# Gated attention in joined units of two blocks, with a second set of buffers, and all scaling of the weights on GpSimd

## The chip, the cores and the metric

The kernel runs on one core of a Trainium2 chip. The metric is the time of one execution in microseconds (us), as the device measures it. A core has five engines, each with its own stream of instructions that it works off in order: TensorE (PE; its weight loads are PEld), VectorE (DVE), ScalarE (ACT), GpSimd (POOL) and SyncE (SP, which issues the DMAs). They meet only at semaphores.

## What is computed

The program runs a transformer of several layers on 512 tokens of width 1024. The change touches one stage, the gated attention of the second layer (`nsa_mixer` in the reference): 16 query heads of width 64 in two groups, and three branches with a gate each. The compressed branch (32 averaged keys) is computed beside the other two, which are full causal attention here, since the selection keeps all blocks of 512 tokens and the window is 512 wide:

```
s_s = jnp.einsum('bqghd,bgqkd->bghqk', qb, k_g) * scale
p_s = masked_softmax(s_s, valid_s[:, :, None]).astype(v_g.dtype)
o_s = jnp.einsum('bghqk,bgqkd->bqghd', p_s, v_g)
...
out = gb[..., 0:1] * o_c + gb[..., 1:2] * o_s + gb[..., 2:3] * o_w
```

## The kernel before

The stage is one loop on each engine, written out by hand, over the list `NSA`: m (8 pairs of heads), x (0 selected, 1 window), b (4 blocks of 128 queries; block b sees b + 1 tiles of 128 keys, so a tile of it is 128 x (b + 1) wide). Two heads (a = 0, 1) go side by side. An iteration over m holds eight blocks, numbered n.

What happens to block n, step by step: TensorE multiplies queries and keys into two of the banks 0 to 3 (L1085, `pe_nsa_logits`); VectorE adds the mask, scales and takes the maximum into `exps` (L2267, `dve_masks`); ScalarE takes exponentials in place and their sum (L1618, `act_exps`); VectorE inverts the sums (L2446) and scales head 0's tile by the inverse and the gate (L2449, both in `dve_nsa_scale`); GpSimd scales head 1's (L2652, `pool_nsa`); TensorE transposes both tiles into banks 4 and 5 (L1100, `pe_nsa_turn`, three steps after the logits); ScalarE copies them to `weights_c` (L1712, `act_nsa_turned`); and when the four blocks of an (m, x) are through, TensorE multiplies them with the values into bank 6 (L1112, `pe_nsa_values`).

Once in an iteration the compressed branch is threaded in, by fixed places in the loop: logits into bank 7 (L1125), on VectorE their maximum and difference (L2461 to L2465, `dve_cmp_logits`), the exponential on ScalarE, the weights on VectorE (L2474 to L2479, `dve_cmp_weights`), two transposes into bank 7 (L1136), a copy to `p_cmpT` on ScalarE (`act_take`), and the values (L1146) into bank 6. The queries of the next m are rotated too: a matmul into bank 7 (L729, `pe_rope`) and three operations on VectorE (L2159 to L2164). Bank 7 is a channel: each writer waits (`emptied7`) until the reader of what was written before has read it. Bank 6 goes to `u` by a copy on ScalarE after the second values of an iteration.

Buffers: the logits banks are reused every second block, so logits n wait for the masks of n - 2 (`c_masked`); `exps` holds one tile for each b and head, so the mask of block n waits for the transposes of n - 4 (`c_t_done`); the transposes wait for ScalarE's copies of the block before (`c_turned0`, `c_turned1`) and for the scaled tiles (`c_scaled`, `c_scaled_1`).

Of the kernel before, what the change touches and what calls it, by code (L numbers as in the profile page):

```python
# [311 lines left out]
def buffers(k):  # L312
# [55 lines left out]
    with ExitStack() as st:  # L368
        exp_buffers(k, st)
# [89 lines left out]
NSA = [(m, x, b) for m in range(8) for x in range(2) for b in range(NB)]  # L459
DA = [(h, b) for h in range(4) for b in range(NB)]  # L460
# [589 lines left out]
def pe_nsa(k):  # L1050


    pe, s = k.pe, k.s
    pe.wait_ge(s["combined"], 2 * (CH_C // 2 + N_C // 2 - 1))
    for step in range(len(NSA) + 5):
        if step < len(NSA):
# [6 lines left out]
        if 0 <= step - 3 < len(NSA):  # L1063
# [24 lines left out]

def pe_nsa_turn(k, n):
    pe, s = k.pe, k.s  # L1090
    m, x, b = NSA[n]
    for a in range(2):
        if n:
            pe.wait_ge(s[f"c_turned{a}"], n)
        if (n, a) == (1, 0):
            pe_keep(k, k.bank[4], 8)
        pe.wait_ge(s[("c_scaled", "c_scaled_1")[a]], n + 1)
        e = sized_tile(k, n, b, a)
        for j in range(b + 1):
            ins = pe.transpose(k.bank[4 + a][:, j * P:(j + 1) * P], e[:, j * P:(j + 1) * P], k.const("ident"))  # L1100
        ins.then_inc(s["c_t_done"], 1)
# [576 lines left out]
def act_nsa(k):  # L1678
    act, s = k.act, k.s
    for step in range(len(NSA) + 5):  # L1680
        m, at = divmod(step, 8)
        n = step - 3
        if 0 <= n < len(NSA):
            act_nsa_turned(k, n)
        if step < len(NSA):
            act_exps(k, step, NSA[step][2], "c_masked", "c_exp_done", sized_tile)
        if m < 8 and at == 0:
            act.wait_ge(s["cmp_shifted"], m + 1)
            act.activation(k.pc, k.pc, ACT.Exp).then_inc(s["cmp_exp"], 1)
        if m < 8 and at == 4:  # L1690
            act_take(k, k.ch7, ("cmpT", m), k.pcT.rearrange("p h q -> p (h q)"), k.ch7.bank[:, 0:2 * P])
        n = step - 4
        if 0 <= n < len(NSA) and n % 8 == 7:
            act_take(k, k.ch6, ("nsa", n // 8), k.u[:, n // 8, :], k.ch6.bank)
# [11 lines left out]
def act_nsa_turned(k, n):  # L1706
    act, s = k.act, k.s
    m, x, b = NSA[n]
    nsa_weights_free(k, act, n)
    for a in range(2):  # L1710
        act.wait_ge(s["c_t_done"], 2 * n + a + 1)
        act.copy(k.ceT[x][a][:, 0:b + 1, b * P:(b + 1) * P],  # L1712
                 k.bank[4 + a][:, 0:P * (b + 1)].rearrange("p (j t) -> p j t", t=P)).then_inc(s[f"c_turned{a}"], 1)
# [700 lines left out]
def dve_nsa(k):  # L2414
    dve, s = k.dve, k.s
    for step in range(len(NSA) + 5):
        m, at = divmod(step, 8)
        if step < len(NSA):
            free = (s["c_t_done"], 2 * (step - 4) + 1, 1) if step >= 4 else None
            dve_masks(k, step, NSA[step][2], causal(k, NSA[step][2]), "c_lg_done", "c_masked", free, SCALE, sized_tile)  # L2420
# [19 lines left out]
def dve_nsa_scale(k, n):  # L2440
# [1113 lines left out]
```

## Time and profile before

| | |
|---|---|
| median of three runs | 2269.31 us (2268.11 to 2269.79) |
| profiled execution | 2269.1 us, its span 2267.8 us |
| PE busy | 98% of the span |
| DVE, ACT, POOL busy | 59%, 25%, 9% |
| granted TensorE clock, mean | 0.999 |

A matmul's busy time includes the time until its result is out, which overlaps the next one; so a busy PE is an engine with work in flight. The stage of the change lies between 855 and 1027 us.

### The profile page before, as it was taken

What the parts mean: (1) busy time and instruction counts of PE and PEld (TensorE: products, weight loads), DVE (VectorE), ACT (ScalarE), POOL (GpSimd) and SP (SyncE); (2) the same over time, 40 slices, a digit from 0 to 9 for tenths busy, and PEclk for the clock granted to TensorE, in tenths of its full rate; (3) what the DMA queues carried; (4) which work ended last, traced back from release to release, by engine and by line L of the source; (5) the groups of instructions that cost most, each with busy time, mean ns of one, the idle gap of its engine ahead of it and who ended that gap; (6) DMA issues with size and microseconds to landing.
All of it is one profiled execution on the core that took longest, in us unless ns stands there. A gap on an engine that the chain in (4) does not pass through costs nothing.

```text
span 2267.8 us, 29576 instructions
## 1 busy us (share of the span) xinstructions
PE 2211.9 (98%) x10990; PEld 1585.1 (70%) x10990; DVE 1344.5 (59%) x3432; ACT 560.3 (25%) x1421; POOL 199.3 (9%) x210
## 2 busy tenths in 40 slices
PE   9999999999999999999999999999999999999997
PEld 7776578888888885558888888888867643333333
DVE  6777756656566667886665666767776522222224
ACT  2223431101001206772110000333572111111111
POOL 0013430000000002330000000000020011111011
PEclk9999999999999999999999999999999999999999
DMA  5211032232223320002222222232205899999997
GB/s 212 75 57 47 13 124 85 83 93 89 79 93 92 116 75 20 1 1 75 76 93 93 78 90 93 76 103 65 65 11 223 347 421 423 423 423 424 424 424 310
DMA packets 60207, 346.54 MB, mean 153 GB/s; under 512 B 9248, under 2 KB 10144, under 8 KB 42208
## 3 DMA queue, kind: packets, MB, share of 16 engines
q1 hardware_dynamic: 55360, 335.03, 39.6%
q0 software_dynamic: 3840, 6.46, 0.8%
q10 hardware_dynamic: 864, 3.15, 0.3%
q8 instruction: 90, 1.47, 0.3%
q14 instruction: 53, 0.43, 0.1%
HBM read 337.59 MB, written 17.30 MB: 156 GB/s over the span
## 4 chain that ended last, share of the span: by engine, by line
PE 86%; DMA 9%; DVE 2%; ACT 1%; issue 1%; SPq 0%; DVEq 0%; POOLq 0%; ACTq 0%
PE bank L634 30%; DMA places<-in_experts 8%; PE bank L640 8%; PE bank L647 8%; PE bank L655 8%; PE bank L3051 6%; PE bank L3059 3%; PE bank L623 2%; PE bank L1100 2%; PE bank L1085 2%; PE bank L1112 2%; PE bank L3008 1%; PE bank L729 1%; PE bank L3024 1%; PE bank L497 1%; PE bank L1307 1%
## 5 line engine op out<-in xcount | busy, mean ns | idle before, releaser
L3051 PE MATMUL bank<-places,xT 128*64 128x512 f32 x824 | 184.0, 594 | 13.9 <-DMA places<-in_experts 13.9
L3260 DVE TENSOR_SCALAR square<-bank,mt 128x256 f32<-128x256 f32 x32 | 15.5, 484 | 288.0 <-ACT rope L3163 288.0
L3051 PEld LDWEIGHTS bank<-places,xT 128*64 128x64 f32 x824 | 59.3, 137 | 133.0 <-issue 117.9
L1961 DVE TENSOR_TENSOR third<-first,bank 128x256 f32<-128x256 f32 x106 | 44.7, 421 | 150.9 <-PE bank L634 150.2
L634 PE MATMUL bank<-u,ring 128*128 128x256 f32 x540 | 130.3, 381 | 1.1 <-DVE y_ab L1995 1.1
L634 PE MATMUL bank<-h,ring 128*128 128x256 f32 x512 | 120.9, 379 | 0.0
L634 PE MATMUL bank<-h_sums,w_sum 128*128 128x256 f32 x512 | 120.9, 379 | 0.0
L2652 POOL TENSOR_SCALAR exps<-exps,small,gates 128x128 f32<-128x128 f32 (+1 forms) x64 | 56.4, 882 | 657.6 <-DVE small L2446 657.6
L634 PEld LDWEIGHTS bank<-u,ring 128*128 128x128 f32 x540 | 101.2, 190 | 17.8 <-issue 3.3
L634 PE MATMUL bank<-u_mlp_sums,w_sum 128*128 128x256 f32 x480 | 113.4, 379 | 0.0
L634 PE MATMUL bank<-u_mlp,ring 128*128 128x256 f32 x480 | 113.4, 379 | 0.0
L1491 ACT ACTIVATE h<-relu 128x512 f32<-128x512 f32 x64 | 40.3, 630 | 273.8 <-DVE relu L2145 250.0
L634 PEld LDWEIGHTS bank<-h,ring 128*128 128x128 f32 x512 | 97.3, 190 | 13.2
L634 PEld LDWEIGHTS bank<-h_sums,w_sum 128*128 128x128 f32 x512 | 97.3, 190 | 13.2
L634 PE MATMUL bank<-exps,w_sum 128*128 128x256 f32 x432 | 102.1, 379 | 0.0
L634 PEld LDWEIGHTS bank<-u_mlp_sums,w_sum 128*128 128x128 f32 x480 | 91.2, 190 | 12.4
L634 PEld LDWEIGHTS bank<-u_mlp,ring 128*128 128x128 f32 x480 | 91.2, 190 | 12.4
L1618 ACT ACTIVATE exps<-exps,small 128x128 f32<-128x128 f32 (+3 forms) x160 | 88.9, 561 | 35.1 <-DVE small L2267 34.6
L3059 PE MATMUL bank<-places,square 128*64 128x512 f32 x392 | 90.0, 598 | 2.4 <-DMA places<-in_experts 2.4
L634 PEld LDWEIGHTS bank<-exps,w_sum 128*128 128x128 f32 x432 | 81.4, 190 | 11.9 <-issue 1.2
L1394 ACT COPY first<-bank 128x256 f32<-128x256 f32 x44 | 16.4, 372 | 275.4 <-PE bank L634 259.4
L640 PE MATMUL bank<-u,ring 128*128 128x256 f32 x312 | 75.8, 382 | 0.0
(556 smaller groups left out, 4406.2 us busy)
## 6 DMA issues: line engine op xcount, KB each, us to landing
places<-in_experts SPq DMA_DIRECT2D x56, 2048.0 KB, 35.1
ring<-in_dense SPq DMA_DIRECT2D x216, 512.0 KB, 4.2
places<-in_experts SPq DMA_DIRECT2D x40, 1024.0 KB, 26.2
x<-in_experts SPq DMA_DIRECT2D x12, 1024.0 KB, 37.8
w<-in_experts SPq DMA_DIRECT2D x10, 1024.0 KB, 32.1
consts<-in_experts SPq DMA_DIRECT2D x10, 1024.0 KB, 32.9
x<-in_experts SPq DMA_DIRECT2D x4, 2048.0 KB, 33.5
consts<-in_consts SPq DMA_DIRECT2D x1, 2310.5 KB, 16.4
```

The costliest lines, as they stand in the source:

```text
L623: ins = pe.matmul(bank, w[:, j, :], x(j), start=i == 0, stop=i == 3)
L634: ins = pe.matmul(bank, w[:, j, :], x(j), start=j == 0, stop=j == 3)
L640: ins = pe.matmul(part[2], a12[:, j, :], tile(2 * j + 1)[:, 0:HT], start=j == 0, stop=j == 3)
L647: ins = pe.matmul(part[4], a22[:, j, :], t4[:, j, :], start=j == 0, stop=j == 3)
L655: ins = pe.matmul(part[3], s4[:, j, :], tile(2 * j + 1)[:, HT:T], start=j == 0, stop=j == 3)
L1085: pe.matmul(logits_bank(k, n, a)[:, 0:P * (b + 1)], k.yc[r, CQ + m, b * P:(b + 1) * P], k.yc[r, (KS, KW)[x], 0:P * (b + 1)], start=True, s ...
L1100: ins = pe.transpose(k.bank[4 + a][:, j * P:(j + 1) * P], e[:, j * P:(j + 1) * P], k.const("ident"))
L1112: ins = pe.matmul(ch.bank[r, j * P:T], k.vcs[x][:, j, r], k.ceT[x][a][:, j, j * P:T], start=False, stop=x == 1 and j == NB - 1)
L1618: act.activation(e, e, ACT.Exp, bias=neg[:, a:a + 1], scale=-1.0, accum_out=total[:, a:a + 1]).then_inc(s[done], 1)
L2652: pool.tensor_scalar(e, e, inv[:, 1:2], k.gt[:, b, q:q + 1], ALU.mult, ALU.mult).then_inc(s["c_scaled_1"], 1)
L3051: ins = k.pe.matmul(bank[a * CAP:(a + 1) * CAP, :], xT[:, kk % 4, kk // 4, :], w[:, (2 * (kk % 2) + a) * EH:(2 * (kk % 2) + a + 1) * EH], ...
L3059: ins = k.pe.matmul(bank[a * CAP:(a + 1) * CAP, :], hT[:, c % 2, c // 2, :], w[:, c % 2 * D + a * T:c % 2 * D + (a + 1) * T], start=c == 0 ...
```

## The change

Three things. First, on TensorE blocks 0 and 1 of each (m, x) are one unit (`NSA_UNITS`), with blocks 2 and 3 as units of their own: their logits go side by side into one pair of banks (block 1 at column 128), and their transposes likewise. An iteration has six steps instead of eight, and every lag (three steps to the transposes, four to the values) counts units. Second, `exps` is ten tiles wide instead of six and holds two sets of a group's tiles (`nsa_tile`), so a mask waits for the transposes of n - 8. Third, GpSimd scales the tiles of both heads, one after the other, and VectorE only inverts. The masks of a unit now wait for all logits of it.

```
@@ pe_nsa @@
-    for step in range(len(NSA) + 5):
+    for step in range(len(NSA_UNITS) + 4):
...
-        m, at = divmod(step, 8)
+        m, at = divmod(step, 6)
...
-        if m < 8 and at == 4:
+        if m < 8 and at == 3:
             pe_cmp_turn(k, m)
-        if m < 7 and at == 5:
+        if m < 7 and at == 3:
             pe.wait_ge(s["scaled"], SCALED["c"] + CQ + m + 2)
             pe_rope(k, k.ch7, ("cq", m + 1), k.yc[:, CQ + m + 1, :])
-        if m < 8 and at == 6:
+        if m < 8 and at == 4:
             pe_cmp_values(k, m)
-        if 0 <= step - 4 < len(NSA) and NSA[step - 4][2] == NB - 1:
-            pe_nsa_values(k, step - 4)
+        if step >= 4 and (step - 4) % 3 == 2:
+            pe_nsa_values(k, NSA_UNITS[step - 4][-1])
@@ pe_nsa_turn @@
+    for a in range(2):
+        for n in NSA_UNITS[u]:
+            m, x, b = NSA[n]
+            if u and n == NSA_UNITS[u][0]:
+                pe.wait_ge(s[f"c_turned{a}"], n)
...
+            pe.wait_ge(s[("c_scaled", "c_scaled_1")[a]], n + 1)
@@ act_nsa @@
+        if 0 <= step - 3 < len(NSA_UNITS):
+            for n in NSA_UNITS[step - 3]:
+                act_nsa_turned(k, n)
+        if step < len(NSA_UNITS):
+            for n in NSA_UNITS[step]:
+                act_exps(k, n, NSA[n][2], "c_masked", "c_exp_done", nsa_tile)
...
-        if m < 8 and at == 4:
+        if m < 8 and at == 3:
             act_take(k, k.ch7, ("cmpT", m), k.pcT.rearrange("p h q -> p (h q)"), k.ch7.bank[:, 0:2 * P])
@@ dve_nsa @@
-            free = (s["c_t_done"], 2 * (step - 4) + 1, 1) if step >= 4 else None
+            unit = NSA_UNITS[nsa_unit(step)]
+            free = (s["c_t_done"], nsa_turns(step - 8, 0), len(unit)) if step >= 8 else None
+            dve.wait_ge(s["c_lg_done"], 2 * (unit[-1] + 1))
@@ dve_nsa_scale @@
     k.inverted.append(own.link(dve.reciprocal(inv, total)))
-    dve.wait_ge(own.sem, k.inverted[n])
-    e, q = sized_tile(k, n, b, 0), 6 * m + 1 + x
-    dve.tensor_scalar(e, e, inv[:, 0:1], k.gt[:, b, q:q + 1], ALU.mult, ALU.mult).then_inc(s["c_scaled"], 1)
@@ pool_nsa @@
-        e, q = sized_tile(k, n, b, 1), 6 * m + 4 + x
         pool.wait_ge(k.dve_own.sem, k.inverted[n])
-        pool.tensor_scalar(e, e, inv[:, 1:2], k.gt[:, b, q:q + 1], ALU.mult, ALU.mult).then_inc(s["c_scaled_1"], 1)
+        for a in range(2):
+            e, q = nsa_tile(k, n, b, a), 6 * m + 3 * a + 1 + x
+            pool.tensor_scalar(e, e, inv[:, a:a + 1], k.gt[:, b, q:q + 1], ALU.mult, ALU.mult).then_inc(s[("c_scaled", "c_scaled_1")[a]], 1)
```

The change moves instructions on every engine; three places follow. The first is TensorE in the middle of an iteration. Before, from the transposes of block 1 on: L1100 are transposes, L1136 the compressed ones, L1085 logits, L729 the rope.

```order
L1100 MATMUL bank<-consts,exps 128x128
L1100 MATMUL bank<-consts,exps 128x128 [waits c_scaled_1,c_turned1]
L1100 MATMUL bank<-consts,exps 128x128
L1136 MATMUL bank<-consts,p_cmp 128x128 [waits emptied7,cmp_weights]
L1136 MATMUL bank<-consts,p_cmp 128x128
L1085 MATMUL bank<-y_c 128x256 [waits c_masked]
L1085 MATMUL bank<-y_c 128x256
L1100 MATMUL bank<-consts,exps 128x128 [waits c_scaled,c_turned0]
L1100 MATMUL bank<-consts,exps 128x128 x2
L1100 MATMUL bank<-consts,exps 128x128 [waits c_scaled_1,c_turned1]
L1100 MATMUL bank<-consts,exps 128x128 x2
L729 MATMUL bank<-y_c,consts 128x512 [waits emptied7,scaled]
```

Of the changed kernel, the same place (L1125 transposes, L1161 the compressed ones, L731 the rope, L1137 the values, L1109 logits):

```order
L1125 MATMUL bank<-consts,exps 128x128 [waits c_scaled,c_turned0]
L1125 MATMUL bank<-consts,exps 128x128 [waits c_scaled]
L1125 MATMUL bank<-consts,exps 128x128
L1125 MATMUL bank<-consts,exps 128x128 [waits c_scaled_1,c_turned1]
L1125 MATMUL bank<-consts,exps 128x128 [waits c_scaled_1]
L1125 MATMUL bank<-consts,exps 128x128
L1161 MATMUL bank<-consts,p_cmp 128x128 [waits emptied7,cmp_weights]
L1161 MATMUL bank<-consts,p_cmp 128x128
L731 MATMUL bank<-y_c,consts 128x512 [waits emptied7,scaled]
L1137 MATMUL bank<-weights_c,y_c 64x512 [waits c_turned1,c_turned0]
L1137 MATMUL bank<-weights_c,y_c 64x512
L1137 MATMUL bank<-weights_c,y_c 64x384 x2
```

The rope now stands directly behind the compressed transposes, which fill the same bank 7, with no logits or transposes between them, and the values stand behind the rope.

The second place is ScalarE at the same point. Before (L1712 copies of transposed tiles, L1618 exponentials of two heads, L1419 the copy of `p_cmpT`):

```order
L1712 COPY weights_c<-bank 128x2x128 [waits c_t_done] x2
L1618 ACTIVATE exps,small<-exps,small 128x128 [waits c_masked] x2
L1419 COPY p_cmpT<-bank 128x256 [waits filled7]
L1712 COPY weights_c<-bank 128x3x128 [waits c_t_done] x2
L1618 ACTIVATE exps,small<-exps,small 128x256 [waits c_masked] x2
```

Now (L1743, L1649, L1444):

```order
L1743 COPY weights_c<-bank 128x128 [waits c_t_done,c_weighed]
L1743 COPY weights_c<-bank 128x128 [waits c_t_done]
L1743 COPY weights_c<-bank 128x2x128 [waits c_t_done] x2
L1649 ACTIVATE exps,small<-exps,small 128x128 [waits c_masked] x2
L1649 ACTIVATE exps,small<-exps,small 128x256 [waits c_masked] x2
L1444 COPY p_cmpT<-bank 128x256 [waits filled7]
L1444 COPY u<-bank 128x512 [waits filled6]
```

The copy of `p_cmpT` came behind one block's copies and one block's exponentials; it now comes behind those of two blocks.

The third place is VectorE from the mask of block 2 to the reciprocal of block 1. Before (L2267 the masks, L2446 reciprocal, L2449 the scaling, L2474 to L2479 the compressed weights), the last rows of it:

```order
L2446 RECIPROCAL small<-small 128x2 [waits c_exp_done]
L2449 TENSOR_SCALAR exps<-exps,small,gates 128x128 [waits dve_chain]
L2474 TENSOR_TENSOR p_cmp<-p_cmp,consts 128x256 [waits cmp_exp]
L2475 TENSOR_REDUCE small<-p_cmp 128x8 [waits dve_chain]
L2476 TENSOR_SCALAR small<-small 128x8 [waits dve_chain]
L2477 RECIPROCAL small<-small 128x8 [waits dve_chain]
L2478 TENSOR_TENSOR small<-small,gates 128x8 [waits dve_chain]
L2479 TENSOR_TENSOR p_cmp<-p_cmp,small 128x256 [waits dve_chain]
L2267 ISA exps,small<-bank,consts 128x512 [waits c_lg_done,c_t_done]
L2267 ISA small 128x1
L2267 ISA exps,small<-bank,consts 128x512 [waits c_lg_done,c_t_done]
L2267 ISA small 128x1
```

Now (L2298, L2479, L2504 to L2509):

```order
L2479 RECIPROCAL small<-small 128x2 [waits c_exp_done]
L2504 TENSOR_TENSOR p_cmp<-p_cmp,consts 128x256 [waits cmp_exp]
L2505 TENSOR_REDUCE small<-p_cmp 128x8 [waits dve_chain]
L2506 TENSOR_SCALAR small<-small 128x8 [waits dve_chain]
L2507 RECIPROCAL small<-small 128x8 [waits dve_chain]
L2508 TENSOR_TENSOR small<-small,gates 128x8 [waits dve_chain]
L2509 TENSOR_TENSOR p_cmp<-p_cmp,small 128x256 [waits dve_chain]
L2298 ISA exps,small<-bank,consts 128x512 [waits c_lg_done,c_t_done]
L2298 ISA small 128x1
L2298 ISA exps,small<-bank,consts 128x512 [waits c_lg_done,c_t_done]
L2298 ISA small 128x1
L2479 RECIPROCAL small<-small 128x2 [waits c_exp_done]
```

Here the scalings are gone and nothing else is moved on VectorE; what moves is TensorE beside it. The transposes of block 1, which wait for the last reciprocal, by way of the scaling, used to have the values of the group before ahead of them on TensorE; in the joined unit they stand ahead of those values.

## Rows read from the trace of the kernel before

**Rows 1.** The page's table of busy time and share of the span by engine.
```profile
PE 2211.9 (98%) x10990; PEld 1585.1 (70%) x10990; DVE 1344.5 (59%) x3432; ACT 560.3 (25%) x1421; POOL 199.3 (9%) x210
```

**Rows 2.** Busy time by engine in the stage: stretch, length, PE, PEld, DVE, ACT, POOL, clock, DMA.
```profile
855.00:1027.00 172.00, 159.66 (x1012) 91.91 (x1011) 132.44 (x493) 126.63 (x408) 56.41 (x64) 1.00 0.01 4
```

**Rows 3.** The chain of waits over one iteration: start, us, what.
```profile
917.02 1.05 PE bank L1125 x8
...
920.16 0.97 PE bank L1100 x6
921.14 0.85 PE bank L1085 x4
921.98 1.03 PE bank L1100 x8
923.01 1.06 PE bank L1085 x4
...
924.57 2.31 PE bank L1112 x16
...
929.88 1.10 PE bank L729 x2
...
932.84 0.89 PE bank L1146 x8
...
937.89 1.05 PE bank L1125 x8
```

**Rows 4.** Groups by line, the stage and its seven later iterations: count, busy, mean, idle before.
```profile
L2449 DVE TENSOR_SCALAR exps<-exps,small,gates 128x128 f32<-128x128 f32 (+1 forms) x64 | 28.7, 449 | 2.4
...
L1100 PE MATMUL bank<-consts,exps 128*128 128x128 f32 x278 | 44.5, 283 | 8.2 <-DVE exps L2449 7.2
```

**Rows 5.** VectorE in order of time: start, us, instruction, idle before in brackets.
```profile
922.12 0.56 DVE L2267 CUSTOM_DVE_ANT_0 exps<-bank,consts 128x384 f32<-128x384 f32 x1 [0.76 <-PE bank L1085]
...
923.08 0.16 DVE L2446 RECIPROCAL small<-small 128x2 f32<-128x2 f32 x1
...
923.54 0.42 DVE L2474 TENSOR_TENSOR p_cmp<-p_cmp,consts 128x256 f32<-128x256 f32 x1
...
925.44 0.68 DVE L2267 CUSTOM_DVE_ANT_0 exps<-bank,consts 128x512 f32<-128x512 f32 x1
...
926.66 0.16 DVE L2446 RECIPROCAL small<-small 128x2 f32<-128x2 f32 x1
```

**Rows 6.** GpSimd in order of time, the stage and the attention stage before it.
```profile
299.18 1.82 POOL L2642 TENSOR_SCALAR exps<-exps,small 128x256 f32<-128x256 f32 x2 [2.16 <-DVE small L2340]
...
920.88 1.04 POOL L2652 TENSOR_SCALAR exps<-exps,small,gates 128x512 f32<-128x512 f32 x1 [0.41 <-DVE small L2446]
...
926.92 0.70 POOL L2652 TENSOR_SCALAR exps<-exps,small,gates 128x256 f32<-128x256 f32 x1 [2.80 <-DVE small L2446]
...
930.13 1.57 POOL L2652 TENSOR_SCALAR exps<-exps,small,gates 128x512 f32<-128x512 f32 x1 [1.13 <-DVE small L2446]
...
1019.02 2.40 POOL L2652 TENSOR_SCALAR exps<-exps,small,gates 128x256 f32<-128x256 f32 x3 [2.96 <-DVE small L2446]
```

**Rows 7.** ScalarE in order of time.
```profile
921.55 0.51 ACT L1618 ACTIVATE exps<-exps,small 128x256 f32<-128x256 f32 x1
...
922.61 1.07 ACT L1712 COPY weights_c<-bank 128x512 f32<-128x512 f32 x2
...
928.06 0.64 ACT L1712 COPY weights_c<-bank 128x256 f32<-128x256 f32 x2
928.59 0.42 ACT L1618 ACTIVATE exps<-exps,small 128x128 f32<-128x128 f32 x1
...
929.37 0.36 ACT L1419 COPY p_cmpT<-bank 128x256 f32<-128x256 f32 x1
```

**Rows 8.** Busy time by engine as above, in the first layer's attention stage; the clock follows POOL.
```profile
292.00:294.00 2.00, 2.00 (x9) 1.20 (x9) 0.69 (x3) 0.81 (x2) 2.00 (x2) 0.68 0.00 0
294.00:296.00 2.00, 2.00 (x13) 1.34 (x12) 1.30 (x6) 1.23 (x5) 1.59 (x2) 0.50 0.04 12
```

More of the change, by code:

```diff
@@ L459 @@
 NSA = [(m, x, b) for m in range(8) for x in range(2) for b in range(NB)]
+NSA_UNITS = [tuple(NB * g + b for b in blocks) for g in range(16) for blocks in ((0, 1), (2,), (3,))]
 DA = [(h, b) for h in range(4) for b in range(NB)]
@@ L1089, in pe_nsa_turn @@
[L1089 to L1101, printed above, removed]
+        if step >= 4 and (step - 4) % 3 == 2:
+            pe_nsa_values(k, NSA_UNITS[step - 4][-1])
@@ new lines, in nsa_unit, with nsa_at, nsa_turns, nsa_logits @@
+def nsa_unit(n):
+    return 3 * (n // NB) + max(0, n % NB - 1)
+def nsa_at(n):
+    return P if n % NB == 1 else 0
+def nsa_turns(n, a):
+    unit = NSA_UNITS[nsa_unit(n)]
+    return 2 * unit[0] + a * len(unit) + unit.index(n) + 1
+def nsa_logits(k, n, a):
+    return k.bank[2 * (nsa_unit(n) % 2) + a][:, nsa_at(n):]
+def pe_nsa_logits(k, u):
+    pe, s = k.pe, k.s
+    if u >= 2:
+        pe.wait_ge(s["c_masked"], 2 * (NSA_UNITS[u - 2][-1] + 1))
+    for n in NSA_UNITS[u]:
+        m, x, b = NSA[n]
+        if n % 8 == 0:
+            pe.wait_ge(s["roped"], ROPED["cq", m])
+        for a in range(2):
+            r = slice(a * HD, (a + 1) * HD)
+            pe.matmul(nsa_logits(k, n, a)[:, 0:P * (b + 1)], k.yc[r, CQ + m, b * P:(b + 1) * P], k.yc[r, (KS, KW)[x], 0:P * (b + 1)],
+                      start=True, stop=True).then_inc(s["c_lg_done"], 1)
@@ new lines, in pe_nsa_turn @@
+def pe_nsa_turn(k, u):
+    pe, s = k.pe, k.s
+    for a in range(2):
+        for n in NSA_UNITS[u]:
+            m, x, b = NSA[n]
+            if u and n == NSA_UNITS[u][0]:
+                pe.wait_ge(s[f"c_turned{a}"], n)
+            if (n, a) == (1, 0):
+                pe_keep(k, k.bank[4], 8)
+            pe.wait_ge(s[("c_scaled", "c_scaled_1")[a]], n + 1)
+            e, at = nsa_tile(k, n, b, a), nsa_at(n)
+            for j in range(b + 1):
+                ins = pe.transpose(k.bank[4 + a][:, at + j * P:at + (j + 1) * P], e[:, j * P:(j + 1) * P], k.const("ident"))
+            ins.then_inc(s["c_t_done"], 1)
@@ L1603, in sized_tile, with nsa_tile @@
     return k.eb.rearrange("p b t -> p (b t)")[:, at:at + P * (b + 1)]
+def nsa_tile(k, n, b, a):
+    at = P * (20 * (n // NB % 2) + 10 * a + b * (b + 1) // 2)
+    return k.ec[:, at:at + P * (b + 1)]
 def soft_columns(k, n):
@@ L1679, in act_nsa @@
     act, s = k.act, k.s
[L1680 to L1689, printed above, removed]
-        if m < 8 and at == 4:
+    for step in range(len(NSA_UNITS) + 4):
+        m, at = divmod(step, 6)
+        if 0 <= step - 3 < len(NSA_UNITS):
+            for n in NSA_UNITS[step - 3]:
+                act_nsa_turned(k, n)
+        if step < len(NSA_UNITS):
+            for n in NSA_UNITS[step]:
+                act_exps(k, n, NSA[n][2], "c_masked", "c_exp_done", nsa_tile)
+                if n % 8 == 0:
+                    act.wait_ge(s["cmp_shifted"], m + 1)
+                    act.activation(k.pc, k.pc, ACT.Exp).then_inc(s["cmp_exp"], 1)
+        if m < 8 and at == 3:
             act_take(k, k.ch7, ("cmpT", m), k.pcT.rearrange("p h q -> p (h q)"), k.ch7.bank[:, 0:2 * P])
-        n = step - 4
-        if 0 <= n < len(NSA) and n % 8 == 7:
-            act_take(k, k.ch6, ("nsa", n // 8), k.u[:, n // 8, :], k.ch6.bank)
+        if step >= 4 and (step - 4) % 6 == 5:
+            act_take(k, k.ch6, ("nsa", (step - 4) // 6), k.u[:, (step - 4) // 6, :], k.ch6.bank)
 def nsa_weights_free(k, eng, n):
@@ L1710, in act_nsa_turned @@
     for a in range(2):
-        act.wait_ge(s["c_t_done"], 2 * n + a + 1)
+        act.wait_ge(s["c_t_done"], nsa_turns(NSA_UNITS[nsa_unit(n)][-1], a))
         act.copy(k.ceT[x][a][:, 0:b + 1, b * P:(b + 1) * P],
-                 k.bank[4 + a][:, 0:P * (b + 1)].rearrange("p (j t) -> p j t", t=P)).then_inc(s[f"c_turned{a}"], 1)
+                 k.bank[4 + a][:, nsa_at(n):nsa_at(n) + P * (b + 1)].rearrange("p (j t) -> p j t", t=P)).then_inc(s[f"c_turned{a}"], 1)
 def act_2_among(k, i):
```

20 lines of the change are left out of this document (5 added, 15 removed).

## The prediction

> **What bounds the kernel now.** I read the page first, for who is busy, and then cut out the one stage that the diff touches. TensorE is in use for 98% of the span [rows 1], so any other engine's saving counts only where TensorE waits for that engine. The stage runs from 855 to 1027 us: 172 us, of which TensorE shows 159.7 us busy, VectorE 132.4, ScalarE 126.6, GpSimd 56.4 [rows 2]. Nothing is moved by DMA here, so no transfer can be late.
>
> The chain of waits says what TensorE does from one iteration over m to the next [rows 3]. An iteration repeats every 20.87 us (917.02 to 937.89, the compressed logits of two iterations). The reader is to see that the pieces are TensorE's own and that only one wait matters, the one that ends at 920.16: VectorE works off the compressed logits and only then scales a 384-wide tile (L2449), for which six transposes wait. Grouped over the seven iterations from 876 on, TensorE waited 7.2 us for that line, 1.03 us each time [rows 3, 4]. So there is about 1.1 us an iteration to win from waits, and the rest is TensorE's own work.
>
> **What the change removes.** Eight scalings per iteration leave VectorE. They are 28.7 us of VectorE's time over the stage, 3.6 an iteration [rows 4]; VectorE was not the bound, but the one wait above loses its last part. The doubled buffer takes away the wait of the masks for the transposes; in the trace the masks' idle time ends with the logits instead (the 0.76 us ahead of the 384-wide mask [rows 5]), so I cost that part at nothing. The cover is that transposes of the block four steps back are always issued before. The joined units save two waiting groups of logits an iteration; the joined logits have as many columns (128 + 256) as a 384-wide block, and I give them its 0.85 us.
>
> TensorE's new order per iteration, without any stall, from the pieces of [rows 3] (six transposes 0.9, two 0.3): logits of blocks 0 and 1 0.85 us, compressed logits 1.05, six transposes 0.9, values 2.31, logits 0.84, transposes 0.9, logits 1.06, transposes 1.03, logits 0.85, transposes 0.9, compressed transposes 0.3, rope 1.10, values 2.31, logits 0.84, transposes 0.9, compressed values 0.89, logits 1.06, transposes 1.03. That is 19.1 us, or 1.7 less than now.
>
> **What it moves onto the path, first place: VectorE's and GpSimd's chain for block 1.** Count from TensorE's start of logits 0 and 1. The values of the group before now stand ahead of the logits of block 2, so these start at 0.85 + 1.05 + 0.9 + 2.31 = 5.1. The mask of block 2 starts 1.0 later, at 6.1 (TensorE 921.14, mask 922.12 [rows 3, 5]). Then VectorE goes on in its order: reciprocal 0.96 after the mask's start, 0.2 for it, the compressed weights 1.90 (923.54 to 925.44), the mask of block 3 1.22 (to 926.66), the reciprocal of block 1, and GpSimd starts 0.26 after that (926.92) [rows 5, 6]. That is 6.1 + 0.96 + 0.2 + 1.90 + 1.22 + 0.26 = 10.6. GpSimd now scales both heads one after the other, 2 x 0.70 [rows 6], to 12.0. The transposes of blocks 0 and 1 end at about 12.4. TensorE could have done them by 5.1 + 0.84 + 0.9 + 1.06 + 1.03 + 0.85 + 0.9 = 10.7. The stall is 1.7 us. Today the values (2.31) stand between and hide this very chain.
>
> **Second place: the rope behind ScalarE.** The rope matmul has moved up to stand directly behind the compressed transposes. Both write bank 7, so the rope waits until ScalarE has copied p_cmpT out. ScalarE does that copy now behind the four copies of the transposed tiles of blocks 0 and 1 and behind the exponentials of two blocks; before, behind one block's of each, with logits and six transposes of TensorE's in between. From 12.4: the last three copies, about 0.1 + 0.2 + 0.64 [rows 7], to 13.3; exponentials of a 128-wide block 0.78 (928.59 to 929.37) and of a 256-wide one 1.06 (921.55 to 922.61), to 15.2; from the start of the p_cmpT copy to the rope 0.51 (929.37 to 929.88), to 15.7 [rows 3, 7]. TensorE was ready at 12.7, so this stall is 3.0 us. Queued behind the rope on TensorE are the values, the next logits and all that follows; VectorE's rope and ScalarE's copy of u wait in turn. From 15.7: rope 1.10, values 2.31, logits 0.84, transposes 0.9, compressed values 0.89, logits 1.06, transposes 1.03: the iteration ends at 23.8 instead of 20.9, so +3.0 us. The end of one iteration does not catch up: the next one's logits wait for nothing that is late.
>
> **The sum of the waits.** Six iterations (m = 1 to 6) pay 3.0 each, 18. The first has nothing to overlap and one values group less: about +1. The last has no rope, keeps the first stall and lands near today's 20. After the last logits GpSimd scales six tiles instead of the three of today's 2.40 us [rows 6]: +2.6, rounded to 3. Together +22.
>
> **The clock.** The granted clock is full in the whole stage today. It fell at a place of the same kind, in the attention stage of the first layer, where TensorE also waits between short groups: the windows from 292 show 0.68 and then 0.50, which is the 1.2 GHz level [rows 8]. Its price by those two rows is 2 x 0.32 + 2 x 0.50 = 1.6 us of full-speed work. In the new order TensorE does only six transposes and the compressed ones between 10.0 and 15.7, a longer pause than any today. I expect one such fall in each of the seven iterations with a rope; part falls into the pause itself and costs nothing, so I take 1.1 us of the 1.6, 7.7 in all.
> The Trainium skill, "TensorE: Matmul & The Clock Gate", on the HAM clock gate, says that idleness throttles the array to 1.2 GHz and that activity releases it; by that rule the clock falls here, by the stage's own rows it would hold. The trace at 292 us agrees with the page.
>
> The profiled execution took 2269.1 us (span 2267.8, 1.3 around it), 0.2 below the median of 2269.31. 2269.1 + 22 + 7.7 = 2298.8, so **2299 us**.
>
> **GpSimd's price** is the term least known. From below: 0.70 for a 256-wide tile, and three back to back in 2.40 us (the same operation) [rows 6]. From above: the attention stage's own scaling, 1.82 for two 256-wide tiles, 0.91 each, and the one of 1.57 for a 512-wide tile where VectorE ropes beside it, against 1.04 without [rows 6]. I take the lower one, since the three back to back are of this very form.
> The Trainium skill, "SBUF — State Buffer", section "Who interferes with whom", says that a VectorE instruction with two SBUF inputs and a GpSimd instruction that reads SBUF exclude each other, and whichever comes first blocks the other. By that, a compressed-weights operation could wait behind a GpSimd scaling, up to 1.04 us more in the first chain and about 7 us over the stage. The trace shows only the half of it in which GpSimd is the longer one (1.57 against 1.04); VectorE's product with two SBUF inputs at 923.54 took 0.42, no longer than its one-input neighbours [rows 5].
>
> **Rivals.**
> - Both stalls as worked out and the clock falls: 2299, by itself 2291 to 2306. Chance 0.50.
> - Both stalls, the clock holds as in today's stage: 2269.1 + 22 = 2291. For it: 1 us pauses leave the clock alone there. Against: the new pause is several times as long. 0.18.
> - GpSimd at the upper price: 0.4 more in the first chain, 0.4 more for the transposes that open the iteration, times 7, and 1.6 in the drain: +7, 2306. 0.15.
> - Faster, the other side: if ScalarE's copy of p_cmpT came in time and the first chain were covered, TensorE's 19.1 us would set the iteration: 8 x -1.7 + 3 = -11, 2258. The point of decision is 1.7 us of stalls an iteration; I find 4.7. For it speaks that VectorE, the engine behind today's wait, loses 3.6 us of work an iteration. Against it speaks the order on ScalarE. 0.09.
> - Stalls of about 1.7 us, so that the change cancels itself: 2269. 0.04.
> - The clock stays low through the rest of each iteration after the pause: 8.1 us of work at half speed, seven times: +57, about 2347. 0.04.
>
> A measurement of this kernel tells a difference from none at about 0.2%, 4.5 us. Faster 0.09, same 0.04, slower 0.87. The range takes in the first three cases with their spread: 2284 to 2310.
>
> **What would show it.** In the changed profile the iteration is near 24 to 25 us. Ahead of the rope matmul TensorE idles 2.5 to 3.5 us until ScalarE's p_cmpT copy; among the transposes of blocks 0 and 1 in the second half it idles 1 to 2 us until GpSimd; the wait for the scaling after the compressed logits is gone. VectorE's busy time in the stage falls by some 29 us and GpSimd's doubles. The granted clock dips once an iteration. The prediction is wrong if ScalarE reaches the p_cmpT copy before TensorE is through with the transposes, if GpSimd's pairs take much other than 1.4 us at 256 wide, or if the clock's share is far from 8 us.

## The result and the profile after

The changed kernel takes 2298.16 us (median of four runs, 2296.26 to 2300.51), the kernel before 2268.71 beside it. The ratio is 1.0127, with a 95% interval of 1.0114 to 1.0140: slower by 1.3%. The forecast was 2299, its range 2284 to 2310. Its profiled execution took 2297.0 us, its span is 2295.7.

The page's table of busy time, which answers to [rows 1], says that TensorE does the same number of instructions and is busy for 97% of a longer span instead of 98%, and that the scaling has gone over: VectorE has 64 instructions and 26.6 us less, GpSimd 64 and 26.3 us more.

```profile
PE 2220.9 (97%) x10990; PEld 1587.5 (69%) x10990; DVE 1317.9 (57%) x3368; ACT 562.1 (24%) x1421; POOL 225.6 (10%) x274
```

Busy time by engine in the stage, and in the two-us windows around one fall of the clock (columns as in [rows 2]). The first row answers to [rows 2], the others to [rows 8]. The stage now ends at 1056.91 instead of 1026.23, where the next matmul is one of L625 (L623 before), and its mean clock is 0.92 instead of 1.00.

```profile
855.00:1056.00 201.00, 167.53 (x1000) 93.36 (x1000) 104.71 (x428) 127.04 (x407) 82.67 (x128) 0.92 0.01 4
939.00:941.00 2.00, 0.00 (x0) 0.00 (x0) 0.00 (x0) 2.00 (x10) 2.00 (x4) 1.00 0.00 0
941.00:943.00 2.00, 1.42 (x2) 0.50 (x2) 0.00 (x0) 0.44 (x3) 0.40 (x1) 0.53 0.03 8
943.00:945.00 2.00, 2.00 (x5) 0.53 (x6) 1.23 (x2) 0.00 (x0) 0.00 (x0) 0.50 0.00 0
945.00:947.00 2.00, 2.00 (x8) 0.71 (x6) 0.15 (x1) 0.00 (x0) 0.00 (x0) 0.50 0.00 0
947.00:949.00 2.00, 2.00 (x13) 0.92 (x10) 0.00 (x0) 0.59 (x1) 0.00 (x0) 0.77 0.00 0
```

What TensorE waited for in the stage (us in total, times, longest): two causes, 19.5 and 11.0 us, hold nearly all of it. The wait of [rows 4] for the scaling after the compressed logits is gone.

```profile
PE bank L731 <- ACT p_cmpT L1444: 19.5, 7, 2.8
PE bank L1125 <- POOL exps L2683: 11.0, 9, 1.3
PE bank L1109 <- DVE small L2298: 1.3, 1, 1.3
```

TensorE in order of time over one iteration (start, us; L1150 are the compressed logits, L1125 transposes, L1109 logits, L1161 the compressed transposes, L731 the rope, L1137 the values). The reader is to see two pauses that the order of before did not have, and that the rope and the values behind the second one take 2.05 and 4.52 us, where the values at 929.06 took 2.37.

```profile
927.36 1.10 PE L1150 MATMUL bank<-k_cmp,y_c 128*128 128x64 f32 x8
928.30 0.83 PE L1125 MATMUL bank<-consts,exps 128*128 128x128 f32 x6
929.06 2.37 PE L1137 MATMUL bank<-weights_c,y_c 128*64 128x512 f32 x16
931.37 0.92 PE L1109 MATMUL bank<-y_c 64*128 64x384 f32 x4
...
935.96 0.33 PE L1125 MATMUL bank<-consts,exps 128*128 128x128 f32 x1
937.60 0.98 PE L1125 MATMUL bank<-consts,exps 128*128 128x128 f32 x5 [1.32 <-POOL exps L2683]
938.41 0.38 PE L1161 MATMUL bank<-consts,p_cmp 128*128 128x128 f32 x2
941.58 2.05 PE L731 MATMUL bank<-y_c,consts 128*128 128x512 f32 x2 [2.78 <-ACT p_cmpT L1444]
943.56 4.52 PE L1137 MATMUL bank<-weights_c,y_c 128*64 128x512 f32 x16
...
953.49 1.10 PE L1150 MATMUL bank<-k_cmp,y_c 128*128 128x64 f32 x8
```

The chain of waits through the same two places answers to [rows 3]. First place: VectorE's reciprocal, then GpSimd, then five transposes. Second place: ScalarE's copies, its eight instructions of exponentials, its copy of p_cmpT, then the rope.

```profile
936.81 0.09 DVE small L2479
...
936.98 0.57 POOL exps L2683
...
937.60 0.99 PE bank L1125 x5
...
938.62 0.82 ACT weights_c L1743 x3
939.43 1.74 ACT exps L1649 x8
941.18 0.27 ACT p_cmpT L1444
...
941.58 2.05 PE bank L731 x2
```

The compressed logits start at 876.96 in the second iteration and at 1028.76 in the eighth, so six periods are 151.80 us, 25.30 each (24.64 to 26.13), against 20.87.

### The profile page after: what moved, and what is told of

Its sections match the earlier page's. It is cut to its first block, busy times and chain, and to the rows that moved or that the text cites. A ratio compares the mean times of both kernels' runs of the same rounds, so it can differ in the third digit from the quotient of the medians.

```text
span 2295.7 us, 29545 instructions
## 1 busy us (share of the span) xinstructions
PE 2220.9 (97%) x10990; PEld 1587.5 (69%) x10990; DVE 1317.9 (57%) x3368; ACT 562.1 (24%) x1421; POOL 225.6 (10%) x274
## 4 chain that ended last, share of the span: by engine, by line
PE 86%; DMA 9%; DVE 2%; ACT 2%; issue 1%; SPq 0%; POOL 0%; DVEq 0%; POOLq 0%; ACTq 0%
PE bank L636 29%; DMA places<-in_experts 8%; PE bank L642 8%; PE bank L649 8%; PE bank L657 8%; PE bank L3082 6%; PE bank L3090 3%; PE bank L625 2%; PE bank L1137 2%; PE bank L1125 2%; PE bank L1109 2%; PE bank L3039 1%; PE bank L731 1%; PE bank L3055 1%; PE bank L499 1%
## 5 line engine op out<-in xcount | busy, mean ns | idle before, releaser
L3082 PE MATMUL bank<-places,xT 128*64 128x512 f32 x824 | 183.8, 594 | 13.6 <-DMA places<-in_experts 13.5
L2683 POOL TENSOR_SCALAR exps<-exps,small,gates 128x128 f32<-128x128 f32 (+3 forms) x128 | 82.7, 658 | 661.4 <-DVE small L2479 661.4
L636 PE MATMUL bank<-u,ring 128*128 128x256 f32 x540 | 130.3, 381 | 1.1 <-DVE y_ab L2026 1.1
L1649 ACT ACTIVATE exps<-exps,small 128x128 f32<-128x128 f32 (+3 forms) x160 | 88.8, 563 | 28.9 <-DVE small L2298 28.9
L2298 DVE CUSTOM_DVE_ANT_0 exps<-bank,consts 128x128 f32<-128x128 f32 (+3 forms) x136 | 59.1, 473 | 48.0 <-PE bank L1109 47.7
L1419 ACT COPY first<-bank 128x256 f32<-128x256 f32 x44 | 16.4, 373 | 275.3 <-PE bank L636 259.3
```

Of the source, the lines that this page charges most:

```text
L636: ins = pe.matmul(bank, w[:, j, :], x(j), start=j == 0, stop=j == 3)
L1649: act.activation(e, e, ACT.Exp, bias=neg[:, a:a + 1], scale=-1.0, accum_out=total[:, a:a + 1]).then_inc(s[done], 1)
L2298: dve.tensor_tensor_reduce(tile(k, n, b, a), logits(k, n, a)[:, 0:w], mask, -scale, 3.0e38, ALU.add, ALU.min, neg[:, a:a + 1]).then_inc(s[ ...
L2683: pool.tensor_scalar(e, e, inv[:, a:a + 1], k.gt[:, b, q:q + 1], ALU.mult, ALU.mult).then_inc(s[("c_scaled", "c_scaled_1")[a]], 1)
L3082: ins = k.pe.matmul(bank[a * CAP:(a + 1) * CAP, :], xT[:, kk % 4, kk // 4, :], w[:, (2 * (kk % 2) + a) * EH:(2 * (kk % 2) + a + 1) * EH], ...
```

## The experiments

All but one start from the changed kernel. The first four tell apart the order at the rope, the clock and GpSimd.

**Values ahead of the rope.** In the step that holds both, TensorE issues the values before the rope matmul.

```
-        if m < 7 and at == 3:
-            pe.wait_ge(s["scaled"], SCALED["c"] + CQ + m + 2)
-            pe_rope(k, k.ch7, ("cq", m + 1), k.yc[:, CQ + m + 1, :])
-        if m < 8 and at == 4:
-            pe_cmp_values(k, m)
         if step >= 4 and (step - 4) % 3 == 2:
             pe_nsa_values(k, NSA_UNITS[step - 4][-1])
+        if m < 7 and at == 3:
+            pe.wait_ge(s["scaled"], SCALED["c"] + CQ + m + 2)
+            pe_rope(k, k.ch7, ("cq", m + 1), k.yc[:, CQ + m + 1, :])
+        if m < 8 and at == 4:
+            pe_cmp_values(k, m)
```

> The changed kernel with one move on TensorE: at the fourth step of an iteration the values of the group before stand ahead of the rope instead of behind it. Theory of two stalls and the clock: the values (2.3 us) cover most of the 2.78 us for which the rope waits for the copy of p_cmpT, in six iterations of seven (the first has no values there), 14 us, and with the pause gone most of the 15 us that the lowered clock costs come back too: 2271 us, 2266 to 2277. Rival, GpSimd's doubled scaling is what costs: the rope's place does not matter, within 4 us of 2298.

It took 2274.45 us, ratio to the kernel before 1.0032 (1.0019 to 1.0044). That is 24 us off the changed kernel, of its 29. TensorE in order of time:

```profile
933.87 0.98 PE L1125 MATMUL bank<-consts,exps 128*128 128x128 f32 x5 [1.32 <-POOL exps L2683]
934.68 0.38 PE L1161 MATMUL bank<-consts,p_cmp 128*128 128x128 f32 x2
934.99 2.37 PE L1137 MATMUL bank<-weights_c,y_c 128*64 128x512 f32 x16
937.85 1.10 PE L731 MATMUL bank<-y_c,consts 128*128 128x512 f32 x2 [0.48 <-ACT p_cmpT L1444]
```

The values now fill the time in which ScalarE works, 2.3 of the 2.78 us of the wait, and rope and values run at full speed: the clock of the stage is 0.98 instead of 0.92. The first pause is as before, 1.32. So the second pause together with its clock is most of the loss. In this trace the clock falls once, from 872 to 879 us, in the first iteration: no values stand there to fill the wait, which is still 2.78. In the six others, with a pause of 1.32 and one of 0.48, it does not fall, so the first pause by itself does not bring it down.

**The copy ahead of the exponentials.** The other way to mend the same place, on ScalarE: it takes p_cmpT out before the exponentials of the next unit.

```
@@ act_nsa @@
+        if m < 8 and at == 3:
+            act_take(k, k.ch7, ("cmpT", m), k.pcT.rearrange("p h q -> p (h q)"), k.ch7.bank[:, 0:2 * P])
         if step < len(NSA_UNITS):
             for n in NSA_UNITS[step]:
                 act_exps(k, n, NSA[n][2], "c_masked", "c_exp_done", nsa_tile)
...
-        if m < 8 and at == 3:
-            act_take(k, k.ch7, ("cmpT", m), k.pcT.rearrange("p h q -> p (h q)"), k.ch7.bank[:, 0:2 * P])
```

> The changed kernel with one move on ScalarE: the copy of p_cmpT ahead of the exponentials of blocks 0 and 1 (1.85 us) instead of behind them. Theory of two stalls: the rope's wait falls from 2.78 to about 0.9 us, 7 x 1.85 = 13 us, and a part of the clock's loss, some 7 us: 2278 us, 2271 to 2286. Rival, GpSimd: the exponentials come later and nothing is won, 2298.

It took 2275.84 us, ratio 1.0038 (1.0024 to 1.0052). The wait for p_cmpT is down from 19.5 us to 7.4 (seven times, 1.05 each in the trace of this kernel), the stage's clock is 0.97: with pauses of 1.3 and 1.05 us it still falls in two of the seven iterations (at 884 and 973 us). Two orders on two engines, one result: it is the position of the rope relative to that one copy, not anything that either step costs.

**Keep the clock up in the pauses.** Both waits stay. TensorE does matmuls on constants in them, whose results nobody reads: four pairs ahead of block 1's transposes, ten pairs ahead of the rope.

```
@@ pe_nsa_turn @@
+            if n > 1 and n % 8 == 1 and a == 0:
+                pe.wait_ge(k.ch7.emptied, k.ch7.n)
+                pe_keep(k, k.ch7.bank, 4)
             pe.wait_ge(s[("c_scaled", "c_scaled_1")[a]], n + 1)
@@ pe_nsa @@
         if m < 7 and at == 3:
+            pe.wait_ge(s["c_masked"], 2 * (NSA_UNITS[step - 1][-1] + 1))
+            pe_keep(k, k.bank[2 * ((step + 1) % 2)], 10)
```

> The changed kernel with matmuls that nobody reads put into TensorE's two pauses (four ahead of the transposes of block 1, ten ahead of the rope), so that it works while it waits. Nothing else moves. Theory: the waits stay as long, and the granted clock stays full; the rope and the values behind it lose their 15.1 us of slowness over seven iterations, less up to 2 us that the fillers overrun: 2284 us, 2281 to 2288. Rival, the clock costs nothing because the waits absorb it: 2298.

It took 2283.86 us, ratio 1.0071 (1.0054 to 1.0088), 14.3 less than the changed kernel. TensorE in order of time (L499 is the filling):

```profile
933.36 1.06 PE L499 MATMUL bank<-consts 128*128 128x128 f32 x8
934.82 0.97 PE L1130 MATMUL bank<-consts,exps 128*128 128x128 f32 x5 [0.41 <-POOL exps L2688]
935.63 0.38 PE L1166 MATMUL bank<-consts,p_cmp 128*128 128x128 f32 x2
935.85 2.40 PE L499 MATMUL bank<-consts 128*128 128x128 f32 x20
938.79 1.10 PE L731 MATMUL bank<-y_c,consts 128*128 128x512 f32 x2 [0.55 <-ACT p_cmpT L1449]
939.82 2.38 PE L1142 MATMUL bank<-weights_c,y_c 128*64 128x512 f32 x16
```

The rope starts as late as before, 3.16 us after the compressed transposes (935.63 to 938.79; 938.41 to 941.58 in the changed kernel). Only the clock differs: 1.00 over the stage. The compressed logits come at 878.58, 901.59, 924.60 and so on, 23.01 apart every time. This run separates the two terms of the sum: 14.3 us of the 29.5 are clock (15.4 by the length of the stage in the two traces), the rest is waiting, the longer end of the stage included.

**Head 0's scaling back on VectorE.** The joined units and the second set stay.

```
@@ dve_nsa_scale @@
+    dve.wait_ge(own.sem, k.inverted[n])
+    e, q = nsa_tile(k, n, b, 0), 6 * m + 1 + x
+    dve.tensor_scalar(e, e, inv[:, 0:1], k.gt[:, b, q:q + 1], ALU.mult, ALU.mult).then_inc(s["c_scaled"], 1)
@@ pool_nsa @@
-        for a in range(2):
+        for a in (1,):
```

> The changed kernel with head 0's scaling back on VectorE, so that GpSimd scales one head as before; joined units and doubled buffers stay. Theory of two stalls: the chain to the transposes of block 1 loses 0.70 us on GpSimd and gains 0.35 on VectorE (the scaling of block 0 ahead of the compressed weights), 0.35 x 8 = 3 us, and the drain loses 2.6: 2293 us, 2288 to 2297; the rope's wait stays at 2.8 us. Rival, GpSimd's doubled scaling is the cost: most of the 29 us come back, under 2283.

It took 2299.76 us, ratio 1.0137 (1.0115 to 1.0159): no gain, where I had expected some 5 us (2288 to 2297). The four runs go from 2294.1 to 2303.9, so the totals alone would not tell 5 us from none; the trace does for the first pause. What TensorE waited for in the stage:

```profile
PE bank L731 <- ACT p_cmpT L1444: 19.5, 7, 2.8
PE bank L1125 <- DVE exps L2482: 11.2, 9, 1.4
```

The first pause has the same length with another name on it. GpSimd saves nothing and costs nothing there: what is late is VectorE's whole row ahead of the scaling (mask, compressed weights, mask), and whoever scales comes behind it.

**The compressed weights a step later.** That row can be shortened for block 1: VectorE works out the compressed weights in the next step of its loop, behind the mask and the reciprocal that block 1 needs.

```
@@ dve_nsa @@
-        if m < 8 and at == 2:
+        if m < 8 and at == 3:
             dve_cmp_weights(k, m)
```

> The changed kernel with VectorE's compressed weights (1.90 us) one block later, behind the mask of block 3 and the reciprocal of block 1, and nothing else moved. Theory: they stand in the chain to the transposes of block 1, whose wait of 1.31 us goes away in each of eight iterations, 10.5 us; the rope's wait of 2.78 us stays. Of the clock's 15 us up to 4 come back, since one of two pauses is gone: 2284 us, 2280 to 2290. Rival, GpSimd itself sets that wait: it stays at 1.3 us and the time at 2298.

It took 2287.03 us, ratio 1.0076 (1.0051 to 1.0101), 11 less than the changed kernel. What TensorE waited for between 870 and 1045 us:

```profile
PE bank L731 <- ACT p_cmpT L1444: 14.5, 6, 2.4
PE bank L1125 <- POOL exps L2683: 2.3, 8, 0.7
```

The first wait falls from 11.0 us to 2.3. The second stays at 2.4 each, and the stage's clock at 0.93. With the first pause nearly gone the clock still falls, so the second one is enough for it.

**Both orders together.** Values ahead of the rope, and the compressed weights a step later.

> Values ahead of the rope (as in e1) and compressed weights one block later (as in e5), GpSimd still scales both heads. Theory: no wait over 0.6 us is left in an iteration but the first one's, TensorE's own 19.1 us and about half a microsecond set it: 8 x 1.2 under today's 20.9 less the longer drain, and the clock full: 2263 us, 2258 to 2268, faster than before the change. Rival, something else in the joined units costs: 2268 or more.

It took 2264.46 us, ratio 0.9971 (0.9958 to 0.9983): the first version that beats the kernel before, by 0.3%. Its profiled execution was the longest of its seven (2275.8); the granted clock was 0.96 between 200 and 400 us and 0.99 up to 855 there, in stages that no edit touches, so I read no more from its trace.

**All three orders**, with the copy ahead of the exponentials as well.

> As e6 and also ScalarE's copy of p_cmpT ahead of the exponentials (as in e2). Theory: the rope's last 0.5 us go too, and the first iteration's 2.8: 2259 us, 2255 to 2264. Rival: the later exponentials hold up VectorE's reciprocals and GpSimd, which has 12.5 us of work an iteration, becomes what is waited for: 2263 or more.

It took 2259.76 us, ratio 0.9961 (0.9948 to 0.9974).

**GpSimd alone, in the kernel before.** Single units and one set of tiles; only the scaling of head 0 goes to GpSimd.

```
@@ dve_nsa_scale @@
-    dve.wait_ge(own.sem, k.inverted[n])
-    e, q = sized_tile(k, n, b, 0), 6 * m + 1 + x
-    dve.tensor_scalar(e, e, inv[:, 0:1], k.gt[:, b, q:q + 1], ALU.mult, ALU.mult).then_inc(s["c_scaled"], 1)
@@ pool_nsa @@
-        e, q = sized_tile(k, n, b, 1), 6 * m + 4 + x
         pool.wait_ge(k.dve_own.sem, k.inverted[n])
...
+        for a in range(2):
+            e, q = sized_tile(k, n, b, a), 6 * m + 3 * a + 1 + x
...
```

> The kernel before the change with one part of the change alone: GpSimd scales both heads, VectorE none; eight steps, one set of buffers. Here each transposition follows its scaling more closely. Theory from the rows of before: the 384-wide tile of the one wait on the chain comes 0.4 us later for head 0 and 0.9 for head 1, the 256-wide ones some 0.3, the second 384-wide one 0.7: about 2 us an iteration and 2.6 in the drain: 2286 us, 2278 to 2292. Rival, since e4 showed GpSimd's doubled work to cost nothing in the joined units, it costs nothing here: 2268.

It took 2275.04 us, ratio 1.0025 (1.0015 to 1.0036), 5.5 more than the kernel before beside it (2269.50). TensorE in order of time:

```profile
923.15 1.16 PE L1100 MATMUL bank<-consts,exps 128*128 128x128 f32 x6 [1.29 <-POOL exps L2650]
```

The wait that the kernel before has for VectorE's 384-wide scaling [rows 3, 4] is there as one for GpSimd's, 1.29 instead of 1.03 in this iteration. Six iterations take 21.72 us each instead of 20.87, so the named wait is not all of it; the transposes behind it are held a little too (1.16 us for six, 0.97 before). I had expected 2 us an iteration and 2278 to 2292 in all, three times too much, because I had added up the durations of single scalings; back to back they are shorter (last section). In that order of the work the move costs 0.25%.

**All three orders, again**, beside the next two on one chip.

> The kernel of e7 again, beside which the next two are to be read: 2260 us, 2257 to 2263.

It took 2257.98 us, ratio 0.9956 (0.9939 to 0.9973). TensorE in order of time, second half of an iteration:

```profile
938.55 0.97 PE L1125 MATMUL bank<-consts,exps 128*128 128x128 f32 x5 [0.23 <-POOL exps L2683]
939.71 0.44 PE L1161 MATMUL bank<-consts,p_cmp 128*128 128x128 f32 x2 [0.19 <-DVE p_cmp L2509]
940.08 2.38 PE L1137 MATMUL bank<-weights_c,y_c 128*64 128x512 f32 x16
942.38 1.12 PE L731 MATMUL bank<-y_c,consts 128*128 128x512 f32 x2
```

Two waits of 0.2 us stand where 1.3 and 2.8 stood, and the rope has none. Second to eighth compressed logits are at 870.73 and 988.07: 19.56 us an iteration, 1.3 less than before, and close to the 19.1 that I had worked out for TensorE without a stall. The clock is 1.00 over the stage.

**The same with head 0's scaling on VectorE.**

> The kernel of e7 with head 0's scaling back on VectorE. Theory that GpSimd's doubled scaling is worth next to nothing either way: VectorE has 16 us of work in an iteration of 19.4 and still keeps up, and the drain is 2.6 us shorter: 2258 us, 2255 to 2262, so within 3 us of e9. Rival, the relief of VectorE is what makes the new order work: 2264 or more.

It took 2260.04 us, ratio 0.9959 (0.9945 to 0.9974), not to be told from the one above. TensorE now waits 5.7 us, seven times, for VectorE's compressed weights.

**The same with one set of tiles.** The masks wait for the transposes of block n - 4 again.

```
@@ nsa_tile @@
-    at = P * (20 * (n // NB % 2) + 10 * a + b * (b + 1) // 2)
+    at = P * (10 * a + b * (b + 1) // 2)
@@ dve_nsa @@
-            free = (s["c_t_done"], nsa_turns(step - 8, 0), len(unit)) if step >= 8 else None
+            free = (s["c_t_done"], nsa_turns(step - 4, 0), len(unit)) if step >= 4 else None
```

> The kernel of e7 with one set of tiles instead of two, so that a mask waits for the transposes of four blocks before. In the joined order these stand behind the logits of the step on TensorE, so each mask starts up to 0.9 us later; the slack behind it is larger in most places. Theory that the second set is worth little: 2262 us, 2259 to 2267. Rival, the second set carries the joined units: 2270 or more.

It took 2267.26 us (median of twelve), ratio 0.9992 (0.9981 to 1.0004): 9 us more than with two sets, just above the range that I had stated, and no longer faster than the kernel before. VectorE's longest wait between 870 and 1020 us, and TensorE's in the stage:

```profile
DVE exps L2298 <- PE bank L1125: 30.1, 20, 3.0
...
PE bank L1125 <- POOL exps L2683: 6.7, 8, 1.2
```

The masks wait for transposes (L1125). In the kernel with two sets the same idle time, 27.5 us, ends with the logits (L1109). A mask that waits for a late transpose makes the next scaling late, and TensorE's wait for it is 6.7 us instead of 2.3. In the two traces, 9.0 us apart, the stage is 7.2 us longer with one set: 4.3 in six periods (20.28 us each instead of 19.56), and most of the rest from one fall of the clock at 1015 us, behind a pause of 1.24 us near the end, in which a group of values takes 3.99 instead of 2.30. The other 1.8 us lie outside the stage.

## Why the prediction was right

**Both places are where it put them**, with the named releaser: block 1's transposes behind GpSimd, the rope behind the p_cmpT copy, once in every iteration, and with the names of what stands behind it. The end of an iteration does not catch up, as it said. The runs without one or the other show that they are the causes: the order at the rope alone gives back 24 us, the compressed weights alone 11, all three orders 40.

**The total hides errors that cancel**, and that it came within 1 us is luck: the waits and the rest of the program came out 9.4 us below the sum, the clock 7.5 above it. In the two profiled executions, whose difference is 27.9 us against 29.7 forecast:

| term | forecast | measured |
|---|---|---|
| waits, iterations 2 to 7 | 18 | 12.9 |
| first iteration, last one and drain | 4 | 2.5 |
| clock | 7.7 | 15.2 |
| the rest of the program | 0 | -2.8 |

The clock's share comes from the rows of TensorE: rope start to next group 1.28 to 1.98 us instead of 1.03, values 2.96 to 4.45 instead of 2.30, 13.6 us over six iterations. In the first, the rope, the logits and the six transposes behind it take 1.6 more than in the run with the filling. Without it a period is 25.30 - 13.6 / 6 = 23.03, which the run with the filling shows directly, 23.01. That is 2.16 over 20.87 and not 3.0. The stage starts 0.1 later, and it ends 30.7 us later.

**The waits were 0.8 us an iteration too long in the sum.** Its steps were off by a little each. TensorE's own order has less in it: six transposes, taken at 0.9 four times, take 0.66 and three times 0.81, which makes 0.5. The stall at the rope is 2.78 and not 3.0. At the first place the profile names 1.32, but the five transposes behind it take 0.99, where five of a group of six that takes 0.81 would take 0.7: TensorE is released by the first of GpSimd's two tiles and held for 0.3 more by the second. Together that is 1.6, where the sum had 1.7 with 1.40 us for the pair. A pair that nothing follows takes 1.10 (GpSimd in order of time):

```profile
927.25 1.10 POOL L2683 TENSOR_SCALAR exps<-exps,small,gates 128x256 f32<-128x256 f32 x2 [1.67 <-DVE small L2479]
```

**The clock was mis-sized**, and this is the step that failed. "Part falls into the pause itself and costs nothing, so I take 1.1 us of the 1.6" took the size of the fall from the attention stage: by the clock of its two windows [rows 8] some 3.3 us at half speed. Here, by windows of 1 us, the clock is at half speed for 34 us in seven falls, 4.9 each, or 2.4 us of full-speed work and not 1.6. And little of it falls into the pause, 0.4 us of the 4.9 on average: in four iterations the fall comes only with the start of the rope or up to 0.7 us after it, in the other three 0.5 to 1.2 us ahead. In the windows above the clock is 1.00 up to 941 us, when TensorE had idled for over 2 us, 0.53 in the next, and low through the rope and nearly all of the values, though TensorE is busy from 941.58 on; it is back to full near 948. The second iteration is the one where most of it lies ahead of the rope, which starts at 891.17 there (columns as in [rows 2]):

```profile
890.00:892.00 2.00, 0.83 (x1) 0.50 (x2) 0.00 (x0) 1.03 (x5) 0.99 (x2) 0.50 0.00 0
```

The cost was 3.1 us in the iteration shown, 1.6 to 3.1 in all seven, 2.2 on average, where the sum had 1.1. By the prediction's own sign, "if the clock's share is far from 8 us", this term was wrong. The rival in which the clock stays low through the rest of the iteration went too far on the other side: in the iteration shown, 3.3 us of the 8.1 us of work ran slow and the rest at full speed.
By the Trainium skill, "TensorE: Matmul & The Clock Gate", on the HAM clock gate, idleness throttles the array to 1.2 GHz and activity releases it. The trace agrees with both halves (0.50 after the pause, full again under work).

**The rest of the program took 2.8 us less, and that was not foreseen.** From the end of the stage on, 1241.6 us in the trace before and 1238.8 in the trace after. Nearly all of it stands in the expert stage, where the last matmuls wait for weights from memory: 18.6 us of waiting for `in_experts` before, 15.8 after. One could take this for time given back because the stage before had ended later and the transfers were ahead. The other traces speak against it: in the eleven experiments these waits are 13.7 to 16.9 us and the rest of the program 1238.2 to 1243.7, and in the two kernels with all three orders, whose stage ends earlier than before (1019.0 and 1015.6 instead of 1026.2), the waits are 15.6 and 16.9 and the rest 1238.2 and 1239.9. So the 2.8 us are a difference between two executions of the size that these show anyway; what sets it is open.

**GpSimd's price** was below even the lower end that the sum took, 1.10 for a pair and not 1.40; the rival with the upper one, 0.91 a tile, has no support in the stage. Nor did GpSimd's busy time in the stage double, as the prediction had said: it went from 56.4 to 82.7 us. VectorE's row was not held up either: from the mask of block 2 to that of block 3 it takes 3.05 us with GpSimd at work from 933.67 to 934.65 in between, where the sum had 3.06 (VectorE in order of time):

```profile
932.45 0.56 DVE L2298 CUSTOM_DVE_ANT_0 exps<-bank,consts 128x384 f32<-128x384 f32 x1 [1.78 <-PE bank L1109]
...
933.49 0.41 DVE L2504 TENSOR_TENSOR p_cmp<-p_cmp,consts 128x256 f32<-128x256 f32 x1
...
935.50 0.68 DVE L2298 CUSTOM_DVE_ANT_0 exps<-bank,consts 128x512 f32<-128x512 f32 x1
```

The Trainium skill, "SBUF — State Buffer", section "Who interferes with whom", has a VectorE instruction with two SBUF inputs and a GpSimd instruction that reads SBUF exclude each other. The 7 us that I had worked out from it as a possible loss are not in this trace; the compressed weights' operations are as long as in [rows 5]. But the row puts it to little test: of the 256-wide products only L2504 overlaps with GpSimd, which starts after it, and L2509 comes when GpSimd is through. Elsewhere the two do slow each other, and on both sides, so "the trace shows only the half of it" in the prediction was a misreading. GpSimd's six tiles of this place take 4.42 us beside VectorE's rope and 3.91 in the last iteration, which has no rope. And in the first layer's attention stage of the kernel before, VectorE's subtraction takes 0.69 beside GpSimd, which works from 278.69 on, and 0.42 while GpSimd is idle (first GpSimd in the kernel after, then VectorE in the kernel before):

```profile
936.98 4.42 POOL L2683 TENSOR_SCALAR exps<-exps,small,gates 128x256 f32<-128x256 f32 x6 [2.33 <-DVE small L2479]
1038.38 3.91 POOL L2683 TENSOR_SCALAR exps<-exps,small,gates 128x256 f32<-128x256 f32 x6 [2.33 <-DVE small L2479]
```

```profile
278.95 0.69 DVE L1913 TENSOR_TENSOR u<-u 128x256 f32<-128x256 f32 x1
312.26 0.42 DVE L1913 TENSOR_TENSOR u<-u 128x256 f32<-128x256 f32 x1
```

**"I cost that part at nothing"** of the second set of tiles holds for the kernel before, where no mask waits for a transpose. In the joined order, with the three steps moved, it does not: the last run puts it at 9 us. Nothing in the forecast of the changed kernel rested on it, since there the set was in place, but as a statement on what the part is worth it was wrong, and in that order the joined units gain something only together with it.

## What to carry to other kernels

When units of work are joined, write out for each engine what now stands ahead of the one short copy or scaling that another engine needs: here GpSimd hardly mattered (5.5 us in the old order, nothing to be measured in the new), and three steps in another order turned +29 us into -11 with the same instructions. A buffer that no engine waits for in the old order may be worth 9 us in the new one, so read its cover again after each change of order. And add to a pause that brings TensorE's clock down what it costs afterwards: here 2.8 us of waiting cost 2.2 more in slow matmuls, and where the order can't be mended, matmuls that nobody reads take that part away.

## What the runs showed of the hardware that I had not expected

- Around each of the seven pauses of 2.8 us the granted clock fell to 0.50, the 1.2 GHz level, and stayed there for 3.3 to 6.4 us in which TensorE was at work. With the pause filled it did not fall (1.00 over the stage); with it cut to 0.5 us in six iterations it fell only in the other one, where it was still 2.8 us (0.98).
- It falls in other stages in some executions and not in others: 0.96 and 1.00 between 200 and 400 us, in two kernels that have the same program there.
- GpSimd and VectorE slow each other only in some places: VectorE's 256-wide subtraction takes 0.42 us with GpSimd idle and 0.69 beside GpSimd's scalings in the attention stage, its 256-wide product in this stage 0.41 us while one starts beside it.
- GpSimd's scalings are shorter back to back: 0.70 us for a 256-wide tile by itself [rows 6], 1.10 for two; all 128 of the stage take 82.7 us.
